# The gate product of two layers: sixteen plain tiles, or four plain tiles and six pairs of seven block products

## The reference

```python
h = h + concat([ya, yb]) @ w_out[i]                    # out stage
e = rmsnorm(p[i] @ w_pe[i], pe_g[i])                   # embedding, 256 -> 2048
h = h + sigmoid(h @ w_pg[i]) * e                       # gate stage: 2048 x 2048
```

## Time and profile before

| | us |
|---|---|
| median of 3 runs | 2524.61 (2524.43 to 2525.24) |
| the profiled execution's own time | 2524.99 |
| its span, first to last instruction | 2523.2 |
| outside the span | 1.8 |

### The profile page before, as it was taken

One profiled execution on the slowest core, in us unless ns is written; L12 is line 12 of the kernel. 1 busy time (PEld: TensorE's weight loads), 2 busy tenths in 40 slices (PEclk: granted clock), 3 DMA queues, 4 the chain that ended last, 5 costly groups with the idle time before them and its releaser, 6 DMA issues.

```text
span 2523.2 us, 40982 instructions
## 1 busy us (share of the span) xinstructions
PE 2515.8 (100%) x15264; PEld 2130.5 (84%) x15264; DVE 1549.4 (61%) x2510; ACT 1066.7 (42%) x1618; POOL 1324.5 (52%) x1668
## 2 busy tenths in 40 slices
PE   9999999999999999999999999999999999999999
PEld 7888888889988888888878899888888888899887
DVE  7977766575462387777665745634654655955722
ACT  6212365643462342223655434634322656545421
POOL 6555554443355555555454434555666776534554
PEclk9999999999999999999999999999999999999999
DMA  7322243248733333223432487233322323388322
GB/s 251 114 92 99 97 123 113 91 144 210 165 108 125 116 118 101 98 94 101 120 114 95 162 188 171 92 133 114 112 98 94 101 92 100 98 188 241 101 95 105
DMA packets 95424, 313.56 MB, mean 124 GB/s; under 512 B 9456, under 2 KB 25584, under 8 KB 92208
## 3 DMA queue, kind: packets, MB, share of 16 engines
q1 hardware_dynamic: 75264, 268.45, 31.6%
q0 software_dynamic: 10368, 37.75, 8.6%
q10 hardware_dynamic: 9648, 5.36, 1.0%
HBM read 297.86 MB, written 16.81 MB: 125 GB/s over the span
## 4 chain that ended last, share of the span: by engine, by line
PE 99%; DMA 0%; ACT 0%; DVE 0%; issue 0%; SPq 0%; POOL 0%; DVEq 0%; ACTq 0%
PE acc L2070 18%; PE acc L2071 18%; PE acc L2072 17%; PE sc L2071 6%; PE sc L2070 6%; PE sc L2072 6%; PE sc L2340 2%; PE sc L2341 2%; PE sc L2342 2%; PE acc L2340 1%; PE acc L2341 1%; PE acc L2342 1%; PE acc L2094 1%; PE sc L2094 1%; PE sc L2096 1%; PE sc L2100 1%
## 5 line engine op out<-in xcount | busy, mean ns | idle before, releaser
L792 POOL TENSOR_TENSOR WL<-raw,WH 128x256 fp32r<-128x256 f32 x1504 | 1195.0, 827 | 907.6 <-ACT WH L852 907.3
L2070 PE MATMUL acc<-XH,WH 128*128 128x512 f32 x1936 | 756.4, 391 | 0.1
L2071 PE MATMUL acc<-XL,WH 128*128 128x512 f32 x1936 | 753.7, 389 | 0.0
L2072 PE MATMUL acc<-XH,WL 128*128 128x512 f32 x1936 | 753.3, 389 | 0.0
L852 ACT ACTIVATE WH<-raw 128x1024 fp32r<-128x1024 f32 x378 | 398.9, 1058 | 795.2 <-PE acc L2072 538.6
L2070 PEld LDWEIGHTS acc<-XH,WH 128*128 128x128 f32 x1936 | 363.4, 188 | 80.5 <-issue 4.9
L2072 PEld LDWEIGHTS acc<-XH,WL 128*128 128x128 f32 x1936 | 363.5, 188 | 76.0
L2071 PEld LDWEIGHTS acc<-XL,WH 128*128 128x128 f32 x1936 | 363.5, 188 | 74.3
L2070 PE MATMUL sc<-XH,WH 128*128 128x512 f32 x640 | 249.0, 389 | 0.0
L2071 PE MATMUL sc<-XL,WH 128*128 128x512 f32 x640 | 249.0, 389 | 0.0
L2072 PE MATMUL sc<-XH,WL 128*128 128x512 f32 x640 | 249.0, 389 | 0.0
(11 more groups left out here) (425 smaller groups left out, 4408.3 us busy)
## 6 DMA issues: line engine op xcount, KB each, us to landing
raw<-in_w SPq DMA_DIRECT2D x416, 512.0 KB, 3.3
raw<-in_w POOLq DMA_DIRECT2D x54, 512.0 KB, 6.2
a<-in_w POOLq DMA_DIRECT2D x18, 512.0 KB, 5.9
a<-in_w SPq DMA_DIRECT2D x16, 512.0 KB, 7.6
h_spill<-H SPq DMA_DIRECT2D x8, 1024.0 KB, 6.1
H<-h_spill SPq DMA_DIRECT2D x8, 1024.0 KB, 8.2
a<-bias_band SPq DMA_DIRECT2D x16, 384.0 KB, 3.7
H<-in_x SPq DMA_DIRECT2D x5, 1024.0 KB, 7.6
```

What stands on the lines that cost most here:

```text
L792: part = pool.tensor_tensor(WL[:, c], raw[:, c], WH[:, c].bitcast(F), ALU.subtract)
L2070: pe.matmul(bank, WH[:, c], xh, start=first, stop=False)
L2071: pe.matmul(bank, WH[:, c], xl, start=False, stop=False)
L2072: return pe.matmul(bank, WL[:, c], xh, start=False, stop=last)
```

## The change

For both layers the gate stage becomes four plain tiles and six pairs of seven block products, by the order `W_STEPS` and its four places. The 16 tiles of the embedding product are stored to DRAM (`e_spill`) in four pieces, since the block sums take their room in `Y`, and come back tile by tile. New h goes to DRAM by tiles (256 KB) and not in four pieces of 1 MB. The plain tiles alternate between two banks, and tanh reads the bank directly. GpSimd makes the low parts of p2 and p7 in the layers. The core of the diff:

```diff
-A_U, KV_U, Z_U, OUT_U, PE_U, PG_U = 48, 8, 32, 8, 4, 32
+A_U, KV_U, Z_U, OUT_U, PE_U, PG_U = 48, 8, 32, 8, 4, 8
+def side_kinds(g):
+    return ("p2",) if g == DEPTH else ("p2", "p7")
...
@@ SP, after the loads of the embedding's units
-                units(u0, PE0, PG0 + 12, skip=skip)
+                units(u0, PE0, PG0, skip=skip)
                 for c in range(4):
+                    e_store(c)
+                    for k in {0: (), 1: (0, 1), 2: (2,), 3: (3,)}[c]:
+                        sp.wait_ge(wl_ready, u0 + (PG0 + k + 1))
+                        load(u0 + (PG0 + RING + k + skip), k)
+                for j in (W_AT["p1", 0], W_AT["p2", 0], W_AT["p1", 1], W_AT["p2", 1]):
+                    name = w_place(*W_STEPS[j])
+                    sp.wait_ge(wl_ready, u0 + PG0 + RING + W_RAW[name] + 1)
+                    sp.dma_start(W_PLACE[name], w[w_unit(ly, *W_STEPS[j])]).then_inc(w_place_in[name], 16)
+                    if j == 0:
+                        e_load(0)
+                sp.wait_ge(sum_tail, 16 * ly + parts_begun(4))
+                e_load(1)
+                e_load(2)
...
+                    for n in SPLITS:
+                        if j == g_done(n) + 6:
+                            h_store(n)
+                        if n + 2 < TAIL_N and j == g_done(n) + kept:
+                            e_load(n + 2)
...
@@ ScalarE, after split_high(4 * ly + 3)
+                for c in range(4):
+                    act.wait_ge(e_kept[c], 16 * (ly + 1))
+                sum_highs(0)
+                third_high(0)
+                third_high(1)
                 prep(u0, PG0 + 2)
+                root(rs[:, :], ly * 4 + 4, 4.0 / D)
+                sum_highs(1)
+                gate(0)
+                sum_highs(2)
                 prep(u0, PG0 + 3)
-                root(rs[:, :], ly * 4 + 4, 4.0 / D)
+                gate(1)
+                sum_highs(3)
+                block_prep(0)
+                square(0)
+                square(1)
+                block_prep(1)
+                gate(2)
...
@@ VectorE, after split_low(4 * ly + 3)
+                def sum_adds(c):
+                    whole, next_ = sum_banks(c)
+                    n = s0 + sums_begun(c)
+                    if c:
+                        dve.wait_ge(sum_tail, s0 + (4 if c < 3 else 6))
+                    if c == 2:
+                        dve.wait_ge(stat_done, ly * 4 + 4)
+                    dve.tensor_tensor(two(whole), att_half(c, 1), h_half(c, 1), ALU.subtract).then_inc(sum_whole, 1)
+                    dve.wait_ge(sum_whole, n + 1)
+                    stt(two(next_), two(whole), -1.0, h_half(c, 0), ALU.mult, ALU.subtract).then_inc(sum_whole, 1)
+                    dve.wait_ge(sum_whole, n + 2)
+                    stt(fourth(c), two(next_), -1.0, att_half(c, 0), ALU.mult, ALU.subtract).then_inc(sum_whole, 1)
...
+                sum_adds(0)
+                third_add(0)
+                third_add(1)
+                sum_lows(0)
+                third_low(0)
+                third_low(1)
+                sum_adds(1)
+                sum_adds(2)
+                sum_lows(1)
+                sum_adds(3)
+                sum_lows(2)
                 dve.wait_ge(root_ready, ly * 3 + 3)
                 did(dve.reciprocal(ers[:, :], rs[:, :]))
+                sum_lows(3)
                 settle()
                 scaled(0)
                 gated(0)
                 scaled(1)
                 gated(1)
+                block_lows(0)
+                sums(0)
+                sums(1)
+                scaled(2)
+                gated(2)
+                for c in range(4):
+                    dve.wait_ge(sum_head, s0 + 10 + c + 1)
+                    dve.tensor_tensor(sums_of(4, True)[:, 2 * c:2 * c + 2, :], fourth(c),
+                                      sums_of(4, False)[:, 2 * c:2 * c + 2, :].bitcast(F), ALU.subtract).then_inc(sum_tail, 1)
+                block_lows(2)
+                sums(2)
+                for j in range(W_N):
+                    for n in SPLITS:
+                        if j == g_done(n) + 4:
+                            sums(n)
+                    if j:
+                        block_outs(j - 1)
+                    if j + 3 < W_N:
+                        block_lows(j + 3)
+                    if j == 0:
+                        scaled(3)
+                        gated(3)
...
+                        if j == g_done(n) + 2:
+                            gated(n)
...
+                        if j == g_done(n) + 1:
+                            scaled(n)
+                    if j >= W_N - 2:
+                        for k in range(2):
+                            next_low(2 * (j - W_N + 2) + k)
+                block_outs(W_N - 1)
+                sums(NT - 3)
+                scaled(NT - 1)
+                next_low(4)
+                next_low(5)
+                gated(NT - 1)
+                sums(NT - 2)
+                for k in range(6, 10):
+                    next_low(k)
...
@@ TensorE
-                quad_tile(n0 + N_PG, u0 + PG0, 0, x0 + 2 * NT)
-                quad_tile(n0 + N_PG, u0 + PG0, 1)
-                stat(4 * ly + 3)
-                for j in (2, 3):
-                    pe.wait_ge(e_out, ly * NT + (NT - 4 + j - 1))
-                    quad_tile(n0 + N_PG, u0 + PG0, j)
-                quads(n0 + N_PG, u0 + PG0, 1)
+                for t in range(PLAIN):
+                    if t >= 2:
+                        pe.wait_ge(g_th, ly * NT + t - 1)
+                    unit(u0 + (PG0 + 2 * t), 2 * t % RING, 0, G[t % 2], None if t else x0 + 2 * NT)
+                    if t == 1:
+                        stat(4 * ly + 3)
+                    unit(u0 + (PG0 + 2 * t + 1), (2 * t + 1) % RING, 1, G[t % 2], None if t else x0 + 2 * NT)
+                for j, (kind, q) in enumerate(W_STEPS):
...
+                        pe.wait_ge(sum_tail, 16 * ly + 10)
...
...
+                    for k in range(CT):
+                        c = slice(w_slot(j) * UW + k * P, w_slot(j) * UW + (k + 1) * P)
+                        pe.matmul(bank, WH[:, c], gate_moving(kind, k, False), start=fresh and k == 0, stop=False, skip_group_check=True)
+                        pe.matmul(bank, WH[:, c], gate_moving(kind, k, True), start=False, stop=False, skip_group_check=True)
+                        last = pe.matmul(bank, WL[:, c], gate_moving(kind, k, False), start=False, stop=k == CT - 1, skip_group_check=True)
```

480 lines of the change are left out of this document (329 added, 151 removed).

## The result

The changed kernel takes 2554.03 us (median of 4 runs, 2552.55 to 2556.73) against 2524.74 of the kernel before: a ratio of 1.0117, 95% interval 1.0099 to 1.0135. It is 29.3 us slower. The forecast was 2528.6 with a range to 2546, so the sign was the likeliest one (slower had 0.44, same 0.42) and the size was missed. The profiled execution took 2555.42 us, its span is 2553.6, 30.4 more than the span before.

The account below looks back on a forecast made before the run. TensorE was taken as the bound, by its matmuls' number and distance. Terms -19.2 + 13.6 + 2.5 + 5.0 + 2.1 = +4.0 us on 2524.99 gave 2529.0, or 2528.6 as median, range 2518 to 2546.

Parts of the forecast that it names:

- slower: Sign of the outcome: a time above 2529.7 us, given a chance of 0.44.
- same: Sign of the outcome: between 2519.6 and 2529.7 us, not told from no change; chance 0.42.
- matmuls: Both gate stages: fewer matmul columns, 174.1 us becoming 164.5 in each layer; -19.2 us in all.
- two first waits: Gate stage start: TensorE waits for the stat's operand and before tile 2; 6.8 us a layer, +13.6.
- products 0 to 7: First block products: p3 waits for VectorE to empty p2's bank; 0.5 and 2.0 us, +2.5 together.
- products 8 to 41 (the middle): Later block products: tight places lose to late DMAs and VectorE; 2.5 us a layer, +5.0.
- the end: After the last product: low part 6 late for the next stage; 0 in the first layer, +2.1 in the second.
- The wait for the first tanh: Tile 2 waits for `gate(0)` behind the block sums; 6.8 us a layer with the stat's wait inside, +13.6.
- The clock: Rival: clock falls in the tile 2 wait, a third of that tile at half clock; 3.6 us a layer, 2535.8; chance 0.08.
- GpSimd, "under half its time": GpSimd gives up 24 low parts and takes p2 and p7, busy under half its time; costed at nothing.
- the DMA engines become the bound: Rival: 19 us more DMA beside the products, which take 133 us a layer; 2547.6; chance 0.17.
- the third rival: The clock falls in the wait before tile 2, 3.6 us more in each layer; 2535.8; chance 0.08.

Follow-up runs that it names:

- small reads: Embedding tiles read back with 8 of 128 partitions, scaling reads h instead; alone on the changed kernel 2548.7 us.
- the copies in the kernel before: Kernel before plus 28 DRAM-to-DRAM copies of 256 KB, two behind each weight load of the recurrent layer's products: 2527.8 us.
- the first run: Changed kernel with ScalarE making the tanh of tile 0 right after the stat's high part, before the block sums' copies: 2554.2 us.
- the filled wait: Changed kernel with 19 more matmuls of 512 columns into a free bank ahead of tile 2: 2550.4 us.
- the start in order: Reordered start (2533.6), with tile 1's read behind low part 0, tiles 2 and 3's behind product 3's weights, fourth sum split during tile 1's load: 2531.6 us.
- the reordered start with small reads: Changed kernel with late stores, p7's low parts on VectorE, earlier tanh, stat after tile 1, reordered start queues, and 8-partition embedding reads: 2527.5 us.

## Why the prediction was wrong

The terms over both layers, as forecast and as read from the changed kernel's profiled execution (30.4 us more span):

| term | forecast | measured |
|---|---|---|
| matmuls | -19.2 | -19.2 |
| two first waits | 13.6 | 14.2 |
| slow matmuls before the products | 0 | 5.1 |
| products 0 to 7 | 2.5 | 4.8 |
| products 8 to 41 (the middle) | 5.0 | 17.9 |
| the end | 2.1 | 2.3 |
| between the stages | 0 | 5.2 |

- **Matmuls, -19.2**: right. Products run at 0.120 us a matmul wherever they don't wait. The gap that the Trainium skill states for an isolated matmul (TensorE: Matmul & The Clock Gate, "Back-to-back issue gap") would make it 0.109; no trace of this case shows that.
- **The wait for the first tanh, +13.6**: right as a reading: 1.89 and 4.69 us, 2.24 and 4.73, 14.2 counted from the starts that were due. Wrong as a price, since its removal gained nothing (2554.2): it covered VectorE's chain, which I had worked out for the first products but not asked what it would do if TensorE came 5 to 9 us earlier.
- **The clock, 0 in the sum, a rival at 0.08**: the step "the granted clock is 1.00" held before, where no wait was over 1.5 us. Behind both waits of 4.7 us, and those of 3.3 and 2.1 at product 37, the clock was lower: 2.1, 2.7, 1.6 and 1.6 us, 8.0 together. Filling one wait in each layer gave back 3.7. By the Trainium skill (TensorE: Matmul & The Clock Gate, "Part 1: The HAM clock gate") sustained work lifts the clock and idling loses it; the trace agrees.
- **The middle, +5.0**: this is the step that failed. From product 8 to the last, the stage lost 10.4 us in the first layer and 7.5 in the second, 17.9 in place of 5.0; some 3 of it are slow matmuls behind product 37. I took the recurrent layer as the nearest row and counted 35 of 40.3 us in the places' chains, at a landing of 6.2 (product 37's 1.1 us to spare was 1.4: it starts at 2306.7). With 7.1 in the median, 8.5 to 9.6 in bursts, there is no margin; 19 us of extra DMA time was in my rival and left out of the sum. Taking the tiles' transfers away gave 13.3 us, and left 1.3 to 1.6 us of loss between products 11 and 37, where the change lost 8.6 and 5.7.
- **The first products, +2.5**: too small as well (4.8), and only the covers hid the rest: where TensorE came 9.6 us earlier, products 0 to 7 took 27.6 to 38.0 us in a layer in place of 23.0, 26.0 and 32.0 with small reads besides.
- **GpSimd, "under half its time", costed at nothing**: in a mean over the stage, but its p7 and p2 follow each other, 7.6 us, and the adding DMAs are issued by the same engine behind them. The name of the cover was missing. Moving p7 to VectorE was worth nothing by itself, since VectorE then has more to do; it moved product 11's margin from 0.5 to 3.2.
- **The rival "the DMA engines become the bound"** (0.17): its products of 133 us came true (133.5), by another way: its share over 0.95 only in places (0.86 in the mean), and the copies in the kernel before reached 0.94 at a cost of 2 us. Its price was 2547.6; with 7.2 of the third rival that makes 2554.8, and that this meets 2554.0 is in part luck: slow matmuls took 5.1 us before the products, not 7.2, and 5.2 us between the stages were in no term. I treated two rivals as alternatives that come together: the stalls of the one bring the other.
- **The end, +2.1**: 0.9 and 1.4 us a layer beyond the pace; right in size, though I had put nothing in the first layer.
- What stays open: the 1.3 us waits in the second layer's attention; how much of the first eight products is the order of VectorE's queue and how much its work beyond the 5 us above; why the first run's gain came back in full and the filled wait's did not. No run left out the transfers and also had the start in order as in the last one; the nearest, the reordered start with small reads, is 1.8 us over the kernel before, so in no run did the 19.2 us of matmuls become a gain.

## What to carry to other kernels

When an order that ran without a wait is borrowed for a stage with more traffic, look up its margins product by product, not its waits: a chain with 1 to 5 us to spare shows none, and a few us of transfers that nobody waits for use it up. A wait that the profile shows is a price only if what it covers is earlier too: before you move work to remove it, ask when the next operand comes. And a wait on TensorE can cost more than its length: the slow matmuls around one of 2.4 us or more took 1.5 to 2.8 us besides in these traces.

## What was not expected of the hardware

- TensorE's clock fell to the lower level around single waits, and the matmuls behind them ran at it for 2.7 to 6.2 us (in the change ten of 512 columns 0.43 us apart, or 17 of 256 columns 0.21 apart; the 6.2 in the run with p7 on VectorE). It did so at every wait of 2.4 us or more in the traces of this case; at waits of 1.8 to 2.3 us it fell in some executions and not in others.
- Over the stages with block products of all runs, adding DMAs of 512 KB took 6.0 us to land in the median when at most one other transfer was issued within 3 us of them, and 7.5 with three (5.4 to 9.8). Tiles of 256 KB in either direction lengthened them: 7.1 us in the change's first layer, 6.7 without the reads, 6.2 without the stores, 5.8 without either.
